# Two blocks in fp32: out-projections begun before their mixer ends, and the late transitions put in another order

## The reference

```python
def first_block(x, ...):                      # post-norm, DEPTH = 2
    for i in range(2):
        x = _layer_norm(ALPHA * x + 0.5 * _swiglu(x, ffn1...), ...)
        m = _pool_mixer(x, ...) if i == 0 else _dilated_attention_mixer(x, w_qkv, w_out)
        x = _layer_norm(ALPHA * x + m, ...)   # the mixer ends in  o @ w_out
        x = _layer_norm(ALPHA * x + 0.5 * _swiglu(x, ffn2...), ...)
    return x

def second_block(x, ...):                     # pre- and post-norm, 16 meta tokens in front
    h = concat(meta, x)                       # 528 tokens
    for l in range(2):
        hn = rmsnorm(h, g[0])
        mix = hgrn2_mixer(hn, ...) if l == 0 else fox_mixer(hn, ...)   # both end in  o @ w_out
        h = h + rmsnorm(mix, g[1])
        h = h + rmsnorm(conv_ffn(rmsnorm(h, g[2]), ...), g[3])
    return h[:, 16:]
```

## Time and profile before

| | |
|---|---|
| median of 3 runs | 3749.17 us (3748.87 to 3750.64) |
| the profiled execution's own time | 3749.11 us |
| its span, first to last instruction | 3747.1 us |
| PE busy | 3603.0 us (96%) |
| DVE / ACT / POOL busy | 1840.5 / 1307.5 / 151.0 us |
| mean granted TensorE clock | 0.976 of full speed |
| HBM read | 308.80 MB, 83 GB/s over the span |

### The profile page before, as it was taken

How to read it: one execution, slowest core, us unless ns; L and a number is a source line. 1 busy time by engine, 2 the same in 40 slices (tenths; PEclk the granted TensorE clock), 3 DMA queues, 4 the chain that set the end, 5 groups by cost and what they waited for, 6 DMA issues and landing times. The chain is left out here.

```text
span 3747.1 us, 56286 instructions
## 1 busy us (share of the span) xinstructions
PE 3603.0 (96%) x22039; PEld 3145.8 (84%) x22039; DVE 1840.5 (49%) x2621; ACT 1307.5 (35%) x1916; POOL 151.0 (4%) x180
## 2 busy tenths in 40 slices
PE   8999899999999999999899989988999989989998
PEld 7888788888888888887888869988999988789997
DVE  3333863335333554545633344554765256757653
ACT  3222542223222333333422234444333234433332
POOL 1000110001000100000100010001000000010001
PEclk9999999999999999999899989989999999999999
DMA  4333222232323322222133322211223211112232
GB/s 134 100 101 102 82 83 94 92 112 77 100 90 107 96 74 73 75 73 74 57 98 98 107 68 69 68 50 57 90 90 101 91 59 45 40 57 90 91 105 73
DMA packets 89978, 313.15 MB, mean 84 GB/s; under 512 B 10832, under 2 KB 15312, under 8 KB 89568
## 3 DMA queue, kind: packets, MB, share of 16 engines
q1 hardware_dynamic: 89344, 308.24, 25.3%
q0 software_dynamic: 480, 2.70, 0.2%
HBM read 308.80 MB, written 2.10 MB: 83 GB/s over the span
## 5 line engine op out<-in xcount | busy, mean ns | idle before, releaser
L622 PE MATMUL ps<-x_hi,w_hi 128*128 128x512 f32 (+3 forms) x3952 | 1340.8, 339 | 12.9 <-DVE x_lo L1934 5.2
L622 PE MATMUL ps<-x_hi,w_lo 128*128 128x512 f32 (+3 forms) x3952 | 1331.7, 337 | 0.0
L622 PE MATMUL ps<-x_lo,w_hi 128*128 128x512 f32 (+3 forms) x3952 | 1327.3, 336 | 0.0
L1649 DVE TENSOR_TENSOR w_lo<-raw,w_hi 128x1024 fp32r<-128x1024 f32 x579 | 705.5, 1227 | 390.0 <-ACT w_hi L1145 380.7
L622 PEld LDWEIGHTS ps<-x_hi,w_hi 128*128 128x128 f32 x3952 | 744.4, 188 | 113.4 <-issue 18.0
L622 PEld LDWEIGHTS ps<-x_hi,w_lo 128*128 128x128 f32 x3952 | 745.3, 189 | 81.3
L622 PEld LDWEIGHTS ps<-x_lo,w_hi 128*128 128x128 f32 x3952 | 743.8, 188 | 80.4
L1145 ACT ACTIVATE w_hi<-raw 128x1024 fp32r<-128x1024 f32 x579 | 603.0, 1051 | 101.2 <-PE ps L622 93.8
L622 PE MATMUL ps<-h_hi,w_hi 128*128 128x512 f32 (+3 forms) x1838 | 622.1, 338 | 6.1 <-issue 3.9
L622 PE MATMUL ps<-h_hi,w_lo 128*128 128x512 f32 (+3 forms) x1838 | 613.1, 334 | 0.0
L622 PE MATMUL ps<-h_lo,w_hi 128*128 128x512 f32 (+3 forms) x1838 | 610.4, 332 | 0.0
(11 more groups left out here) (234 smaller groups left out, 2926.4 us busy)
## 6 DMA issues: line engine op xcount, KB each, us to landing
raw<-wstream SPq DMA_DIRECT2D x579, 512.0 KB, 3.3
res<-xT SPq DMA_DIRECT2D x8, 256.0 KB, 7.6
out<-res SPq DMA_DIRECT2D x8, 256.0 KB, 2.1
invc<-consts POOLq DMA_DIRECT2D x1, 1024.0 KB, 5.3
bias<-consts POOLq DMA_DIRECT2D x1, 1024.0 KB, 5.1
g_chunk<-consts POOLq DMA_DIRECT2D x1, 264.0 KB, 3.0
g_keep<-consts POOLq DMA_DIRECT2D x1, 256.0 KB, 3.1
par<-params SPq DMA_DIRECT2D x1, 232.5 KB, 7.4
```

The lines of the kernel that those rows point to most:

```text
L622: m = pe.matmul(ps[:, bank, 0:n], w[:, slot, wt, :], x[:, k, c0:c0 + n], start=first and q == 0, stop=last and q == 2)
L1649: dve.tensor_tensor(w_lo[:, slot], raw[:, slot], w_hi[:, slot].bitcast(F32), ALU.subtract)\
```

## The change

1. **Early begin of two out-projections** (`early=RING` for the ones behind `attend1` and `hgrn`). PE issues the blocks of the first four units of the out-projection, for the tiles that are already there (k = 0 to 6), in the pieces of the mixer's last head; the last block (k = 7) of each follows at the start of the out-projection. Four accumulations are open at once, in banks 0 to 3 behind `attend1` and 0 to 7 behind `hgrn`. For this `attend1` splits `att` pair by pair into `att_hi` and `att_lo` (in place), units 2 and 3 are split before the last head is done, and the other splits look RING ahead in place of AHEAD = 2.
2. **Squares in four buffers** in `project2` (two in `pair[:, 1]`, two in `sums[:, 0]`; `renorm` keeps two).
3. **Their sums in blocks.** Half 0: behind each of the last eight steps of the projection (where `halved` is 4), or all behind it (where it is 1). Half 1: in one block, in all four transitions, between `first_units`' pass with `x_lo` of half 0 and its half 1.
4. **Another order on ACT and DVE** in the transition: tile scalings, late tiles and the four splits are laid out by hand; `rstd` of half 1 is taken after the second `x_hi`; DVE scales half 1 only after all of half 0's next input, and adds it to `res` itself, in place of POOL.

```diff
+def begin(st, n, ks):
+    src, s_in, in0 = out_source(st)
+    if ks[0] == 0:
+        pe.wait_ge(s_lo, st["u0"] + n + 1)
+    for k in ks:
+        pe.wait_ge(s_in, in0 + k + 1)
+        for a, c0, cols in halves(st["tok"]):
+            m = products(early_bank(st, n) + a, (st["u0"] + n) % RING, k, src, ...)
+    if ks[-1] == KD - 1:
+        m.then_inc(s_unit, 1)
 def project(st):
-    for n in range(full):
+    for n in range(st["early"]):
+        begin(st, n, range(KD - 1, KD))
+    for n in range(st["early"], full):
...
-                if h and st.get("outs") and steps >= 20 and steps % 2 == 0 and squared < KD:
+                if h and st.get("outs") and halved > 1 and steps > KD * halved - KD:
                     squares_of(st, 0, [squared])
...
     if st.get("outs"):
-        late.append(lambda j, k: squares_of(st, 1, [k]) if j == st["lead"] // 2 else None)
+        between.append(lambda: squares_of(st, 1, range(KD)))
 def attend1(st):
-    for t in (3, 9, 27):
-        second_part(KD - 1, t)
+    second_part(KD - 1, 3)
+    pe.wait_ge(s_evac, nxt["t0"])
+    begin(nxt, 0, range(0, 3))
+    second_part(KD - 1, 9)
+    begin(nxt, 0, range(3, 7))
+    begin(nxt, 1, range(0, 4))
+    second_part(KD - 1, 27)
+    begin(nxt, 1, range(4, 7))
+    for n in (2, 3):
+        begin(nxt, n, range(KD - 1))
 def hgrn(st):
+    begin(nxt, 0, range(0, 3))
     mean_square(KD - 2)
+    begin(nxt, 0, range(3, 6))
+    begin(nxt, 1, range(0, 3))
     turn_and_score(KD - 1)
+    begin(nxt, 1, range(3, 6))
     state_steps(KD - 1)
+    for n in range(2):
+        begin(nxt, n, range(6, 7))
     outputs(KD - 1)
-    mean_square(KD - 1)
+    begin(nxt, 2, range(0, 2))
+    mean_square(KD - 1, 3)
+    begin(nxt, 2, range(2, 7))
+    begin(nxt, 3, range(KD - 1))
 # DVE, project2 with outs and halved == 4
+for q, tiles in enumerate(((0, 1, 2), (3, 4, 5), (6, 7), ())):
+    for k in tiles:
+        normalise(0, k)
+    late_tile(q)
+    split(nxt + q, (nxt + q) % RING)
+def second_half():
+    for k in range(KD + 1):
+        if k < KD:
+            normalise(1, k)
+        if k:
+            add(k - 1)
 # ACT, the same place
+for q, squares in enumerate(((0, 1), (2, 3, 4), (5, 6, 7), ())):
+    late_tile(q)
+    split(nxt + q, (nxt + q) % RING)
+    for k in squares:
+        square(st, 0, k)
+next_input(st, other)
```

More of the change, by code:

```diff
@@ L196, in plan @@
     ffn1(1, 0, lead=4)
-    add("attend1", dict(u=9 * KD, t=9 * KD, x=KD))
-    project("x", 0, (KD,), 1.0, 1, 1, lead=4)
+    add("attend1", dict(u=9 * KD, t=9 * KD))
+    project("att", 0, (KD,), 1.0, 1, 1, lead=4, early=RING)
     ffn1(1, 2, lead=2)
@@ L435, in build @@
         A = {name: sem("s_a_" + name) for name in (
-            "vtr", "val", "score", "add", "max", "turn", "top", "wide", "x", "exp", "pv", "rec", "att")}
+            "vtr", "val", "score", "add", "max", "turn", "top", "wide", "x", "exp", "pv", "rec", "att", "hi", "lo")}
         s_mixed = sem("s_mixed")
@@ L638, in unit @@
                         between(k)
-            late = []
+            late, between = [], []
             def first_units(st, count, tok):
@@ L671, in first_units @@
                         product(0, j, k, w_hi, lo, False, k == KD - 1)
+                for f in between:
+                    f()
+                between.clear()
                 if st["t0"]:
@@ L711, in project @@
                         if h == 0:
-                            pe.wait_ge(s_evac, st["t0"] + n - RING + 1)
+                            pe.wait_ge(s_evac, st["t0"] + min(n - RING + 1 + (st["early"] > 0 and tok == S), full))
                         k0 = 0
@@ L1330, in attend1 @@
                                 weights(p - 1, True)
+                            if j == 5:
+                                high(p - 1)
                         take(p, j)
+                nxt = follower(st)["u0"]
                 weights(KD - 1, False)
+                split(nxt + 2, (nxt + 2) % RING)
                 weights(KD - 1, True)
-                for k in range(KD):
-                    act.wait_ge(A["att"], k + 1)
-                    act.activation(x_hi[:, k, META:T], att[:, k, :], ACT.Copy).then_inc(s_xhi, 1)
+                split(nxt + 3, (nxt + 3) % RING)
+                high(KD - 1)
             def glu2(st):
@@ L1930, in attend1 @@
                 shift(KD - 1, True)
+                nxt = follower(st)["u0"]
+                for u in (nxt + 2, nxt + 3):
+                    split(u, u % RING)
                 normalise(KD - 1)
-                for k in range(KD):
-                    dve.wait_ge(s_xhi, st["x0"] + k + 1)
-                    dve.tensor_tensor(x_lo[:, k, META:T], att[:, k, :], x_hi[:, k, META:T].bitcast(F32),
-                                      ALU.subtract).then_inc(s_xlo, 1)
+                low(KD - 1)
             def glu2(st):
@@ L2042, in next_input @@
                                               ALU.subtract).then_inc(s_xlo, 1)
[L2043 to L2045 removed]
+                    if h == 0 and other:
+                        other()
             def renorm(st):
@@ L2369, in add_mixed @@
             def add_mixed(st):
-                for h in range(2):
+                for h in range(1 if st["outs"] else 2):
                     c = half_cols(st["tok"], h)
```

174 lines of the change are left out of this document (120 added, 54 removed).

## The result

The changed kernel takes **3700.62 us** (median of 4 runs, 3699.90 to 3700.97) against 3749.4 us before: ratio 0.987, 95% interval 0.9856 to 0.9884. The forecast was 3702, the range 3690 to 3720. The profiled execution took 3700.97 us, its span is 3699.2 us at a mean granted clock of 0.983, against 3747.1 us at 0.976 before.

A forecast was written before the change was run, and what follows sets the result against it. PE bounds the kernel (busy 96%); only its 144 us idle and half-clock time can be won. 5.3 + 18.3 + 11.8 + 11.7 + 6.0 - 1.3 - 4.8 = 47.0 us off 3749.1: 3702 us, range 3690 to 3720.

The forecast's parts named there:

- part 5: renorm's transition: half 1's squares in a block with two buffers leave a path uncovered, 1.3 us lost (0.5 to 2.6).
- the clock: Restarts at half clock behind PE's idle waits, five at 0 to 1.7 us each; 4.8 us lost.
- Part 1: End of attend1: early matmuls fill PE's idle times, the burst of evacuations gives back 6.1 us; 5.3 us won.
- Part 2: End of hgrn: early blocks remove idle time (some 13 us) and half clock (5 to 6); 18.3 us won.
- the filled stretch stays at full clock: End of hgrn: with PE kept busy the throttle stays released; the half-clock share of the gain is 5 to 6 us.
- Part 3: Transitions behind hgrn's and fox's out-projections (four late tiles): half 1 starts at 38.2 us; 11.8 and 11.7 us won.
- part 4: Conv feed-forward's transition (one late tile): DVE's detours go, x_hi every 0.75 us; 6.0 us won.
- (a): Transitions: squares at steps 25 to 32 wait for ACT, giving 14 us in place of 29.5; 3718 us, chance 0.2.
- (b): End of hgrn: early blocks delay the last head's chain, keeping 12 us there; 3708 us, chance 0.13.
- (d): Transitions: blocks stall PE, DVE's additions double and half clock persists; slower, about 3753 us, chance 0.03 with half-way cases.
- (c): Less lost than charged: no half-clock restart, attend1's evacuation burst drains at 3.0 us a tile; 3694 us, chance 0.17.

The follow-up runs named there:

- Experiment 1: The changed kernel without either early begin (behind attend1 and behind hgrn), att still split head by head; 3716.96 us, ratio 0.9915.
- 4: The changed kernel with DVE's scalings of half 1 put back between the inputs of half 0 in the transitions; 3707.6 us, ratio 0.9888.
- 6: The changed kernel with half 0 of the three transitions back in the old order on ACT and DVE, sums from step 20; 3714.96 us, ratio 0.9905.
- experiment 5: The changed kernel with half 1's residual additions back on POOL in the three transitions; 3700.94 us, ratio 0.9869.
- experiment 7: The changed kernel with two square buffers instead of four in the three transitions; 3701.88 us, ratio 0.9874.
- experiment 8: The changed kernel with half 1's squares in a block in renorm too, with its two buffers; 3704.25 us, ratio 0.988.
- 11: The changed kernel with staggered early units behind attend1: k = 7 of units 0 and 1 ahead of unit 3's last four steps; 3696.85 us, ratio 0.9857.
- 2: The changed kernel without the early begin behind hgrn, keeping the one behind attend1; 3716.0 us, ratio 0.9913.
- experiment 3: The changed kernel with the three old transitions back (two square buffers, squares between products, additions on POOL), both early begins kept; 3727.98 us, ratio 0.9944.
- experiment 10: The changed kernel with the block of half 1's squares ahead of half 0's x_lo products instead of behind them; 3692.1 us, ratio 0.9838.

## Why the prediction was right, and where it was not

The time was right (3702 against 3700.6) and the mechanisms of parts 2 to 4 were the ones that the traces show. That it came so near is in part luck. Parts 1 to 4 were put at 53.1 us and gave 48.3, 4.8 too much; part 5 and the clock were put at 6.1 us lost, while nothing came of the first and the clock cost 1.9 us behind the places counted. One term had nearly the right size for the wrong reason, one stood for something that the change does not do, and the clock was priced in the wrong places.

- **Part 1, 5.3 us forecast, 4.7 measured.** The chain was as drawn: `weigh` 6.7 us at full clock, four units at once, evacuations every 3.47 us (3.6 forecast), one wait of 4.49 us ("about 4.5"). But I gave the gain to the early begin and counted the splitting of `att` head by head as costing nothing. Experiment 1 shows the reverse: the kernel without early blocks reaches the next stage 4.0 us sooner than the kernel before (5.2 counted from `weigh`), and the early blocks add almost nothing until their ends are staggered. A change with two parts that share a place was costed as one.
- **Part 2, 18.3 forecast, 15.2 measured.** The step that failed is "the filled stretch stays at full clock". PE's idle time there was 2.2 us (1.5 forecast), yet the granted clock was 0.57 over 7.9 us behind the wait of 1.40, most of it at the lower level, 1.2 GHz. The same instructions behind the same wait ran at 1.00 in seven of the experiments' kernels and then took 2.9 us less, which is nearly all of the shortfall. The Trainium skill ("TensorE: Matmul & The Clock Gate", Part 1) says that activity releases the throttle, and from that I took the filled stretch as safe; the traces bear it out in those seven kernels and not in the changed one and three others (0.57), so the term should have been 15 to 18.
- **Part 3, 11.8 and 11.7 forecast, 11.6 and 11.4 measured**, and **part 4, 6.0 forecast, 5.4 measured**. (By the prediction's own figures, 49.7 less 38.2, the second is 11.5.) From the start of the first late tile to half 1 it is 38.8 us (38.2 forecast), with no wait over 0.6 us for half 0's squares, an `x_hi` every 0.75 us and a new wait of 2.57 us (2.5 forecast). The statement that these belong to the order is shown by experiments 4 and 6 (7.0 and 14.3 us). That additions on DVE matter was not claimed, and they don't by themselves (experiment 5); four buffers are worth 2.8 us (experiment 7).
- **Part 5, 1.3 lost.** There is no such term: `renorm` is untouched. Had the block been there, it would have cost 3.6 (experiment 8).
- **Clock, 4.8 lost.** In the first transition half 1 ran at a granted clock of 0.87 behind its wait of 2.57 us and took 13.5 us for 96 products; the kernel before, without that wait, took 11.9. That is 1.6 us, and the two other transitions lost 0.3 together. It is not sure either: behind the same wait half 1 was as slow in experiments 1, 4, 5 and 11, and 1.5 us faster in 2, 6, 7 and 8. Behind `attend1`, from the end of the 4.49 us wait to the next stage's first wait (1836.98), it is 26.6 us, against 25.1 in experiment 11, whose clock is 1.00 there (from 1807.65, less its two waits of 0.40): 1.5 us, which are inside the 4.7 of part 1. So the places that I had named cost 3.4 us and not 4.8, while the 2.9 us in `hgrn` had no term.
- **Rivals.** (a) is excluded by the squares of half 0, which wait for nothing at steps 25 to 32; (b) by `hgrn`'s 0.79 and 1.40 us; (d) by the clock of 0.90 to 0.96 in the transitions, and by the time. (c) came nearest, by what was not lost at the restarts, but its drain of 3.0 us a tile did not come.

What stays open: why the clock fell at the end of `hgrn` in four kernels and not in seven with the same instructions there. They differ in other places and in when the stretch starts (2508 to 2519 us); each was seen in one profiled execution, and no run separated the start time from anything else. Open too is what moved the 1.0, 1.3, 2.2 and 1.5 us outside the change. And `att`'s splitting was never undone alone: its share follows from the kernel without early begins against the kernel before, which also differ in how far ahead the weights are split.

## What to carry to other kernels

When work is put in front of a wait to fill it, look where the work it feeds will pile up: four accumulators finished together cost 4.5 us of waiting that four finished one after another did not. When steps are gathered into a block, the latency behind the block's last step needs a cover, and one may stand next to it: here the block cost 5.1 us against squares between the products, and moving it ahead of 32 independent products won 8.8. And undo each part of a change alone and together: the old order made 4.6 us of waits alone, POOL's additions none, and the kernel with both (and half 0's old order) has 11.85; a part costed at nothing carried the gain of its neighbour. Last, before a difference of 1 to 3 us is put down to an edit, look whether the clock moved somewhere that the edit does not touch.

## What the runs showed of the hardware

- DVE and POOL slow each other: a subtraction of 128x264 on DVE takes 0.42 us alone and 0.97 beside POOL's additions (experiment 3), a scaling 0.48 and 0.98 (experiment 5). An addition on POOL takes 0.75 us while DVE is idle and 0.94 beside those scalings (experiment 5).
- The granted clock fell to 0.57 over 7.9 us of uninterrupted matmuls behind a wait of only 1.40 us, in four kernels, and stayed at 1.00 in seven others behind the same wait. Behind a wait of 2.57 us half 1 took 14.1 us to the next wait's end in five kernels and 12.6 in four. Of executions of one kernel too: that of experiment 10 took 3686.7 to 3693.7 us at mean clocks of 0.986 to 0.984.
